# Loading the first weight chunk in two halves, moving the row table in the queue, and waiting per part of the transposed input

## What is computed

```python
h = rms_norm(x, norm_mix)                   # layer 0
z = gelu(h @ w_in); u, v = split(z)         # "v" and "u" products
v = layer_norm(v); y = (u * (w_s @ v + b_s)) @ w_out   # "mix", gate, "out"
x = x + y
t = rms_norm(x, norm_ffn)
q = (t @ w_query)                           # 8 heads x 2 halves of 128
s = q . sub_keys                            # 128 scores for each half
idx = top16 of the sums of both top16s      # 16 experts per head and token
a = gelu(expert_u[idx] . t)
x = x + sum(softmax(scores) * a * expert_v[idx])
```

## Time and profile before

| | |
|---|---|
| median of the timed runs | 1755.8 us (1754.67 to 1757.43, n = 3) |
| the profiled execution's own time | 1754.86 us |
| its span, first to last instruction | 1753.0 us |
| mean granted clock of TensorE | 0.813 |
| busy: PE, DVE, ACT, POOL | 76%, 62%, 38%, 36% |
| moved by the DMA engines | 721.53 MB, 604.02 MB of it by the 576 gathers |
| mean rate over the span | 412 GB/s |

### The profile page before, as it was taken

How to read it: one execution, slowest core, us unless ns; L and a number is a source line. 1 busy time by engine, 2 the same in 40 slices (tenths; PEclk the granted TensorE clock), 3 DMA queues, 4 the chain that set the end, 5 groups by cost and what they waited for, 6 DMA issues and landing times.

```text
span 1753.0 us, 23629 instructions
## 1 busy us (share of the span) xinstructions
PE 1330.9 (76%) x8378; PEld 643.0 (37%) x8378; DVE 1082.1 (62%) x2636; ACT 658.0 (38%) x2139; POOL 628.0 (36%) x580
## 2 busy tenths in 40 slices
PE   8999998998858777786754688688786676666744
PEld 7995555544525433451100255244441111111100
DVE  1369567554756565556677756767567666666454
ACT  2125444234434223343343523326343433433343
POOL 0024334333334223343343333334343444444441
PEclk9999999999979987887665699898896766666655
DMA  9989999999999999999999999999999999999996
GB/s 367 413 345 400 418 420 421 421 421 421 420 421 421 421 421 421 417 421 421 422 411 422 413 421 421 420 421 414 421 408 409 421 421 421 421 421 415 421 410 279
DMA packets 101766, 721.53 MB, mean 412 GB/s; under 512 B 12304, under 2 KB 13072, under 8 KB 14448
## 3 DMA queue, kind: packets, MB, share of 16 engines
q0 software_dynamic: 82944, 604.02, 83.3%
q1 hardware_dynamic: 17904, 115.27, 16.1%
q10 hardware_dynamic: 800, 0.74, 0.1%
HBM read 718.46 MB, written 1.52 MB: 411 GB/s over the span
## 4 chain that ended last, share of the span: by engine, by line
DMA 55%; PE 26%; DVE 7%; ACT 6%; issue 2%; SPq 2%; POOL 1%; DVEq 0%; ACTq 0%; POOLq 0%
DMA uvring<-expert_uv_dram,idx 54%; PE psum L762 10%; PE psum L773 8%; DVE uvring L1483 5%; PE psum L929 3%; PE psum L817 2%; ACT diag L1100 1%; POOL uvring L715 1%; ACT wgt L1096 1%; DMA wring<-w_chunks_dram 1%; SPq L672 1%; ACT a_gelu L1088 1%; PE psum L781 1%; PE psum L950 1%; PE psum L912 1%
## 5 line engine op out<-in xcount | busy, mean ns | idle before, releaser
L1483 DVE SCALAR_TENSOR_TENSOR uvring<-uvring,xn 128x1024 f32<-128x1024 f32 x576 | 704.9, 1225 | 552.7 <-DMA uvring<-expert_uv_dram,idx 531.5
L715 POOL DMA_INDIRECT uvring<-expert_uv_dram,idx x576 | 627.8, 1090 | 1101.1 <-PE psum L762 859.1
L762 PE MATMUL psum<-uvring,diag 64*64 64x512 f32 x4096 | 688.1, 765 | 301.0 <-ACT diag L1100 279.1
L1088 ACT ACTIVATE a_gelu<-a_raw 128x1 f32<-128x1 f32 x576 | 116.4, 202 | 880.9 <-DVE uvring L1483 872.7
L762 PEld LDWEIGHTS psum<-uvring,diag 64*64 64x64 f32 x4096 | 131.1, 155 | 733.1 <-ACT diag L1100 639.6
L773 PEld LDWEIGHTS psum<-xT,wring 128*128 128x128 f32 x1440 | 197.2, 200 | 67.8 <-issue 60.8
L773 PE MATMUL psum<-xT,wring 128*128 128x160 f32 (+1 forms) x1440 | 215.5, 306 | 2.6 <-DMA wring<-w_chunks_dram 2.6
L1100 ACT ACTIVATE diag<-twin,wgt 128x64 f32<-128x64 f32 x512 | 178.1, 348 | 48.9 <-ACT wgt L1096 1.9
L1096 ACT ACTIVATE wgt<-a_gelu,gate 128x1 f32<-128x1 f32 x576 | 169.7, 295 | 20.9
L754 PE MATMUL psum<-uvring,diag 128*32 128x256 f32 x512 | 67.1, 630 | 93.4 <-ACT diag L1100 83.6
L773 PEld LDWEIGHTS psum<-xT,kept 128*128 128x128 f32 x512 | 67.6, 197 | 21.6 <-issue 20.8
(11 more groups left out here) (156 smaller groups left out, 853.3 us busy)
## 6 DMA issues: line engine op xcount, KB each, us to landing
wring<-w_chunks_dram SPq DMA_DIRECT2D x68, 1024.0 KB
uvring<-w_chunks_dram SPq DMA_DIRECT2D x23, 1024.0 KB, 15.1
kept<-w_chunks_dram SPq DMA_DIRECT2D x10, 1024.0 KB, 13.8
uvring<-expert_uv_dram,idx POOLq DMA_INDIRECT x576
uvring<-ln_gain_dram SPq DMA_DIRECT2D x1, 1024.0 KB, 26.7
uvring<-ln_bias_dram SPq DMA_DIRECT2D x1, 1024.0 KB, 27.0
keys<-sub_keys_dram SPq DMA_DIRECT2D x2, 512.0 KB, 22.4
arena<-w_chunks_dram SPq DMA_DIRECT2D x1, 1024.0 KB, 11.4
```

The costliest lines, as they stand in the source:

```text
L715: pool.indirect_dma_start(uvring[:, n % RING, :], None, expert_uv, bass.IndirectOffsetOnAxis(ap=idx[t][:, i:i + 1], axis=0),).then_inc(uv_ ...
L762: mm = nc.tensor.matmul(acc[64 * j:64 * j + 64, 512 * i:512 * (i + 1)], diag[64 * i:64 * i + 64, n % DIAGS, :], row[64 * i:64 * i + 64, D ...
L1088: nc.scalar.activation(a_gelu[:, c:c + 1], a_raw[:, c:c + 1], ACT.Gelu_apprx_tanh).then_inc(gelu_done, 1)
L1483: nc.vector.scalar_tensor_tensor(out=uvring[:, slot, 0:D], in0=uvring[:, slot, 0:D], scalar=1.0, in1=xn[t][:, :], op0=ALU.mult, op1=ALU.mu ...
```

## The change

It does these things:

- SP loads chunk 0 in two transfers: the rows of weights that belong to products 0 to 3 (512 KB, with a semaphore of its own), then those for 4 to 7.
- The row table is no longer ACT's third transfer. SP issues it behind chunk 9, ahead of the layer norm rows.
- The first v product asks for each quarter of the transposed x as it comes to it, and for the second half of chunk 0 only ahead of its fifth product.
- In pass 0, the transposes of quarters 0 to 2 of the new x go one half column group earlier, between the two halves of the next out product. The first six products of query blocks 0 and 1 become steps of their own ("q head"), placed on both sides of the last quarter's transposes. They ask for quarters up to 2 only. The last two products of each block stay where the block was.
- ACT runs a one-element square root at the start, once DVE has set the constant it reads.
- The planner gets a rule for late `exp` and `recip` steps.

```diff
--- before.py
+++ after.py
@@ -221,12 +221,15 @@
         for h in range(2 if l == 0 else 1):
             gated = ("gate", n, 4 * h + 3) if l == 0 else ("conv gate", n)
             out.append(("PE", ("out", l, c, h, tiles[0]), row, [gated]))
+            if n == 0 and h == 0 and c:
+                quarter("ffn", c - 1, ("add", 0, c - 1, 0))
             if 2 in tiles:
                 out.append(("PE", ("oq", l, c, h), 0.6, [gated]))
         out.append(("DVE", ("add", l, c, tiles[0]), 0.85, [("out", l, c, 1 - l, tiles[0])]))
-        for q in range(4) if n == 0 else ():
-            if q == c - 1 or q == c == 3:
-                quarter("ffn", q, ("add", 0, q, 0))
+        if n == 0 and c == 3:
+            out.append(("PE", ("q head", 0), 1.4, [("xT read", 0, "ffn", 0, 2)]))
+            quarter("ffn", 3, ("add", 0, 3, 0))
+            out.append(("PE", ("q head", 1), 1.4, [("xT read", 0, "ffn", 0, 2)]))
         if 2 in tiles:
             out.append(("ACT", ("oq read", l, c), 0.5, [("oq", l, c, 1 - l)]))
             out.append(("PE", ("of", l, c), 0.5, [("oq read", l, c)]))
@@ -382,6 +385,8 @@
                     elif hurry:
                         mine = mine[::-1]
 
+                if mine and mine[-1][0][1][0] in ("exp", "recip") and p > due(mine[-1][0][1]) + 3:
+                    mine = mine[::-1]
                 tied = (e == "PE" and mine and mine[0][0][1][0] in ("vq", "oq")
                         and plan[e][p] and plan[e][p][-1][0] in ("v", "out"))
                 if not mine or credit[e] <= 0.1 and not hurry and not tied:
@@ -576,6 +581,7 @@
         bias_landed = sem("bias_landed")
         x_landed = [sem(f"x_landed{t}") for t in range(NT)]
         half_landed, gains_landed, ffn_gain_landed = sem("half_landed"), sem("gains_landed"), sem("ffn_gain_landed")
+        first_half_landed = sem("first_half_landed")
         rstd_ready, first_normed = sem("rstd_ready"), sem("first_normed")
         const_landed, ln_landed = sem("const_landed"), sem("ln_landed")
         rows_landed, keys_landed = sem("rows_landed"), sem("keys_landed")
@@ -660,8 +666,13 @@
 
             sp.dma_start(x[0][:, 0:512], x_tok[0:P, 0:512]).then_inc(half_landed, 16)
             sp.dma_start(x[0][:, 512:D], x_tok[0:P, 512:D]).then_inc(x_landed[0], 16)
-            for n in range(PREFETCHED):
+            for half in range(2):
+                ks = slice(4 * half, 4 * half + 4)
+                sp.dma_start(place_of(0)[0][:, ks, :], w_chunks[0][:, ks, :]
+                             ).then_inc((first_half_landed, place_of(0)[1])[half], 16)
+            for n in range(1, PREFETCHED):
                 load_chunk(n)
+            sp.dma_start(table, rows).then_inc(rows_landed, 16)
             for row in range(2):
                 sp.dma_start(ln_full[:, row, :], (ln_gain, ln_bias)[row].partition_broadcast(P)).then_inc(ln_landed, 16)
             for dst, src in (
@@ -765,14 +776,16 @@
                                                   start=first, stop=last)
                 mm.then_inc(v_tensor, 1)
 
-            def blocks(n, name, b, act, cols):
+            def blocks(n, name, b, act, cols, ks=range(KD)):
                 w = chunk(n, {"u": 8, "bch": 0, "q": 24 if n < 2 else 16}[name] + b // 2)
                 key, j = (name, n, b), b % 2
-                open_group(key)
-                for k in range(KD):
+                if 0 in ks:
+                    open_group(key)
+                for k in ks:
                     mm = nc.tensor.matmul(bank(key, WIDTH[n]), w[:, k, j * P:(j + 1) * P], act[:, k, 0:cols],
                                           start=(k == 0), stop=(k == KD - 1))
-                mm.then_inc(group_done, 1)
+                if KD - 1 in ks:
+                    mm.then_inc(group_done, 1)
 
             def quarter_sums(key, at, act, w, start, stop):
                 b0 = G[key][1] * 512 + at
@@ -809,11 +822,18 @@
                 elif kind == "v":
                     _, c, t = k
                     n = 0 if t == 0 else 1
-                    w = chunk(n, c)
-                    if c == 0:
-                        scalar_has_read(("xT", 0, "mix", t, 1 if t else 3))
+                    w = chunk(n, c) if n or c else place_of(0)[0]
+                    if c == 0 and t == 1:
+                        scalar_has_read(("xT", 0, "mix", t, 1))
                     open_group(k)
                     for kk in range(KD):
+                        if (c, t) == (0, 0) and kk % 2 == 0:
+
+                            scalar_has_read(("xT", 0, "mix", 0, kk // 2))
+                            if kk == 0:
+                                pe.wait_ge(first_half_landed, 16)
+                            elif kk == 4:
+                                chunk(n, c)
                         mm = nc.tensor.matmul(bank(k, WCOLS, ROWS[t]), (xT if t else raw_T)[:, kk, 0:ROWS[t]],
                                               w[:, kk, :], start=(kk == 0), stop=(kk == KD - 1))
                     mm.then_inc(group_done, 1)
@@ -937,7 +957,12 @@
                     _, n, b = k
                     if b == 0:
                         scalar_has_read(("xT", n // 2, "ffn", PASSES[n][1][-1], 1 if n else 3))
-                    blocks(n, "q", b, xT, WIDTH[n])
+                    blocks(n, "q", b, xT, WIDTH[n], range(6, KD) if n == 0 and b < 2 else range(KD))
+                elif kind == "q head":
+
+                    if k[1] == 0:
+                        scalar_has_read(("xT", 0, "ffn", 0, 2))
+                    blocks(0, "q", k[1], xT, WIDTH[0], range(6))
                 elif kind == "s":
                     _, l, t, first, count = k
                     n = 2 * l + (t > 0)
@@ -1118,7 +1143,9 @@
 
             act.dma_start(ident[:, :], ident_c).then_inc(ident_landed, 16)
             act.dma_start(gains[:, :, :], gains_c).then_inc(gains_landed, 16)
-            act.dma_start(table, rows).then_inc(rows_landed, 16)
+
+            act.wait_ge(step, 2)
+            nc.scalar.activation(warm[:, :], eps[0:1, 0:1], ACT.Sqrt)
             for k in PLAN["ACT"][-1]:
                 do(k)
             for p in range(TURNS):
```

## The result

| | before | after |
|---|---|---|
| median of the timed runs, side by side on one chip | 1756.67 us (1754.53 to 1759.3, n = 20) | 1759.74 us (n = 20) |
| ratio after / before, 95% interval | | 1.0015 [1.0009, 1.0022] |
| the profiled execution: own time, span | 1754.86, 1753.0 us | 1760.27, 1758.5 us |

The change makes the kernel 3.1 us slower. One of the 20 executions of after took 5253.96 us, at a mean granted clock of 1.0; the ratio leaves it out, and without it the median is 1759.56 us. The loss is inside the 0.2% that the prediction called no change, but the interval leaves out 1, and 1759.7 lies above the predicted range. The forecast of 1756.4 was wrong.

The account below looks back on a forecast made before the run. The prediction took DMA bandwidth of the 576 gathers as the bound. Clock +1.7 and heads -0.25 made the first gather 1.45 us later; a hole absorbed 0.85, leaving +0.6: 1756.4 us, range 1752.6 to 1758.9.

Parts of the forecast that it names:

- the price of the move for chunk 10: Table issued in SP's queue ahead of chunk 10: claimed to cost zero, chunk 10 still landing at 48.1 us.
- the extra issue for the second half: SP's additional issue for chunk 0's second half, 0.43 us: claimed hidden under a 9 us backlog.
- the clock's fall: PE's wait at chunk 10 grows to 2.6 us, the clock halves, and products behind it come 1.7 us later.
- The second failed step: Table in SP's queue: claimed its bytes were moved before chunk 10 in the old order too; price zero.
- The first product: Start of the kernel: first product at 8.3 us, 2.3 us earlier (1.2 to 4.6), from halves and table.
- The rival that chunk 10 comes earlier: The table's move gives every chunk back 1.3 us at the start; time 1754.2 us, chance 0.18.
- The heads: Before the first query: they fill 1.1 us of PE's idle time, but the first gather gains only 0.25 us.
- The planner's rule: Rule for late exp and recip steps: claimed to move nothing in ACT's and DVE's plans; zero.
- The hole that was to take up 0.85 us: DMA hole from 136.5 to 144 us, 1.6 us of empty time: absorbs 0.85 us of the first gather's delay.
- The base: Starting time of the forecast: the median of three runs, 0.9 us above the profiled execution's 1754.86 us.
- "Slower": Wait at chunk 10 over 3 us, clock low for two stretches, 3.6 us lost; time 1758.8 us, chance 0.10.
- The likeliest case: The main forecast: wait at chunk 10, clock falls, stream shifted by +0.6 us; time 1756.4 us, chance 0.50.

Follow-up runs that it names:

- tiny_extra: Kernel before with one 8 KB transfer, into a tile nobody reads, added behind chunk 9 in SP's queue; 1757.75 us, ratio 1.0006.
- pieces_late: Kernel after with the eight w_s pieces issued behind chunk 11 instead of ahead of chunk 10; 1757.2 us, ratio 1.0004.
- ahead_alone: Kernel before with chunks 10 and 11 issued ahead of the bias rows and w_s pieces; 1754.57 us, ratio 0.9986.
- heads_ahead: Kernel before with the query heads, and chunks 10 and 11 issued ahead of the bias rows and w_s pieces; 1754.63 us, ratio 0.9988.
- all_ahead: Kernel after with chunks 10 and 11 issued ahead of the bias rows and w_s pieces, the table behind chunk 20; 1752.0 us, ratio 0.997.
- before_again: Kernel before, unchanged, profiled on another execution; 1757.09 us, ratio 1.0001.
- halves_only: Kernel before with chunk 0 in two transfers, the waits per part and the early square root; 1759.54 us, ratio 1.0018.
- table_only: Kernel before with only the table moved from ACT to SP's queue behind chunk 9; 1759.09 us, ratio 1.001.
- table_back: Kernel after with the table back as ACT's third transfer; 1759.83 us, ratio 1.0018.
- filler: Kernel after with 24 extra products on PE ahead of the first product on chunk 10, outputs unaffected; 1758.45 us, ratio 1.0007.
- halves_both: Kernel before with chunk 0 in two transfers, PE waiting for both ahead of its first product, no early square root; 1758.26 us, ratio 1.0011.
- heads_only: Kernel before with the query heads and earlier transposes alone, without the planner's rule; 1756.24 us, ratio 0.9998.

## Why the prediction was wrong

**The step that failed** is the price of the move for chunk 10, put at zero, with its twin that the extra issue for the second half "lies under a backlog of 9 us". Both held chunk 10 at 48.1; it came at 52.2. Behind them stood the reading of the earlier trace rows, that chunk 10 comes when the bytes ahead of it have been moved, with the rate taken as given: a share of 0.98 was taken for a full queue. But the same window says 335 GB/s where a full queue gives 421. The bytes ahead of chunk 10 are the same in every kernel of the second table, but for 8 KB in `tiny_extra`; the rate at which they go is not, and that is what the change lowered. Chunk 10 landed 7.9 to 9.0 us after its issue in all kernels with the old order, at 48.1 to 52.2. That the issue alone sets the landing doesn't follow: in `pieces_late` it was issued 0.65 us ahead of the earlier trace rows and landed 1.7 us behind. That chunk 10's lateness is what costs the time, `ahead_alone`, `heads_ahead` and `all_ahead` show: with chunk 10 early they are 2.3, 2.0 and 4.9 us faster than before.

The first gather of after is 5.7 us later than in the shown execution: chunk 10 is 4.1 of it, the clock 2.0, and the heads give 0.4 back. But the medians are 3.1 us apart, and the shown execution was a fast one. Against `before_again`, whose own time is near the median, the first gather is 3.4 us later: chunk 10 is 1.8 of it, the clock 2.0, the heads again -0.4. So in the usual execution the term put at zero is worth 1.8 us, and the clock's fall, which the prediction did price, is as large. These are one execution of each.

**The second failed step** is the table's, that "its bytes were moved before chunk 10 in the old order too". Their number is the same, but in their new place the rate is nearly halved for 4 us, 2.1 us' worth by 36 us. `pieces_late`, where the hole is mended and chunk 10 still lands at 49.8, shows that this costs something by itself.

**The clock** was right in kind and in size: a fall behind the wait, some 4 us of products at half pace, 2.0 us lost where 1.7 was forecast. As a law it was wrong. The 26 of 26 waits of 2 us and more were those of one execution; `before_again` has one of 2.36 us behind which the clock held, and `halves_only` one of 3.71 us.

**The first product** was forecast at 8.3 (6.0 to 9.4) and came at 8.99, but its two terms were mis-sized against each other. The sum gave the table 0.6 us and the halves 1.7. With chunk 0 whole and the table on ACT's queue PE starts at 10.62 to 11.15 (six kernels), with the table gone at 9.16 (`table_only`). With the halves it starts at 10.20 and 9.74 (`table_back`, `halves_only`), and with both at 8.31 to 9.10 (`pieces_late`, `filler`, after, `all_ahead`). So the table's leaving is worth 0.6 to 2.0 us and the halves 0.1 to 1.4. In `halves_both`, where PE waits for both halves, they are there only at 11.54. That the table's leaving brings chunk 0 forward at all fits two queues that take turns, which is what the Trainium skill says in "DMA: Bandwidth & Descriptors", section "Queues, rings and completion order".

**The rival that chunk 10 comes earlier** was half right. The table does cost more than its bytes (up to 2.0 us of chunk 0 where 0.26 MB are 0.6). But the change puts it where it is still ahead of chunk 10, and there it costs about as much again, 2.1 us of rate. The first 10 us move no more than before, 252 against 259 GB/s: without the table they move 278 (`table_only`), and the halves take that back.

**The heads** went as forecast: they fill PE's idle stretches, the root moves later against the last out product, MAX8 loses its wait, and the first gather gains 0.35 to 0.45 us (0.25 forecast) and not 1.1. In time that can't be seen: 1754.63 against 1754.57 us with and without them. The planner's rule was forecast at zero, and no run has it alone.

**The hole that was to take up 0.85 us** seems not to have. The sum let the stream follow PE's later steps and not the first gather. But from the first gather to the end after takes 1641.98 us and the two executions of before 1642.14 and 1642.06, so 0.1 to 0.2 us was taken up. Over all kernels this stretch spreads by 1.9 us, so the term is small here and not excluded.

**The base.** The forecast stood on the median of three runs, 1755.8 us; side by side before has 1756.67. So 0.9 us of the 3.3 us between 1756.4 and 1759.7 is the base, and the forecast change of +0.6 us compares with 3.1 measured.

**The rivals.** "Slower" had the sign, the long wait and nearly the time (1758.8), and was given 0.10. Its cause was another: an early start of PE, at 6.0 us, where PE started at 8.99 and the chunk was late. To that extent its time came out by luck. One thing in it came true, a fall that begins in the wait (49.5 us) and so lies half on idle time; it cost 2.0 us and not 3.6. The likeliest case and the slower one share the wait at chunk 10, and the prediction held its end fixed in both. The shown execution helped in this: with 0.30 us of waiting it looked as if chunk 10 came just in time, and the second execution has 1.29.

**What stays open.** Why the table's transfer nearly halves the rate was not tried; the trace shows busy engines that move little. It goes to 64 partitions (`x[2][64:P, :]`) where the chunks go to 128; the same table to 128 would have told. Neither was tried what exactly holds SP back, the number of transfers or of their parts. With a further transfer at the head, much of what the w_s pieces begin later is one long issue of `pick` ahead of them: 3.0 to 6.9 us where it is 0.4 to 1.6 in the two executions of before and in `heads_only`. What the halves cost, the slower start or the later issues, isn't separated either: against `before_again` chunk 10 lands 1.2 us later in the three kernels, and the 0.4 to 0.5 MB less of the first 10 us would make 0.9 to 1.2 us of it. In `all_ahead` the halves and the late table came together, so their shares in the 2.6 us over `heads_ahead` aren't separated. The costs of the table and the halves do not add up: +2.4 and +2.6 (or +1.6) alone, +3.1 together, each known to about 1.6 us.
